# A fp32 decoder layer on one core: stored permuted identity for the keys, new first loads and first rotation, row-block-first end

## What is computed

```python
h = rmsnorm(x, attn_norm)
qkv = einsum('bsd,de->bse', h, w_in)            # (256,1024) x (1024,3072)
q, k = rope(q), rope(k)
o_moba = moba_attention(q[:8 heads], ...)       # one block of 256 keys: causal attention
o_dil = dilated_mixture(q[8 heads:], ...)       # three dilated windows, mixed by denominators
mixed = concat(rmsnorm(o_moba), rmsnorm(o_dil))
x = x + mixed @ w_out
h = rmsnorm(x, ffn_norm)
x = x + (silu(h @ w_gate) * (h @ w_up)) @ w_down
out = rmsnorm(x, final_norm)
```

## Time and profile before

| what | us |
|---|---|
| median of three runs (lowest, highest) | 311.64 (311.19, 312.02) |
| the profiled execution: its own time | 311.84 |
| its span, first to last instruction | 309.9 |
| TensorE busy with matmuls | 301.3 (97%) |
| VectorE busy | 200.7 (65%) |
| ScalarE busy | 170.8 (55%) |
| GpSimd busy | 10.3 (3%) |
| TensorE's share of the chain that ended last | 96% |
| moved by DMA | 61.59 MB, 199 GB/s on average |

### The profile page before, as it was taken

The page is one execution under the profiler, slowest core; times in us unless marked ns, Lnnn a source line. Parts: engine busy times, 40 slices in busy tenths (PEclk is TensorE's granted clock), DMA queues, the critical chain, the costliest instruction groups (busy, mean ns, idle before and its releaser), DMA issues.

```text
span 309.9 us, 4293 instructions
## 1 busy us (share of the span) xinstructions
PE 301.3 (97%) x1430; PEld 246.1 (79%) x1430; DVE 200.7 (65%) x323; ACT 170.8 (55%) x294; POOL 10.3 (3%) x24
## 2 busy tenths in 40 slices
PE   7999999999999999999999999999999999999991
PEld 3788877788888988888888888888888888888880
DVE  3677979997877388855757374656565555555425
ACT  4785563968678458746453443526354444444224
POOL 0001000000020020200000000000000000000002
PEclk9999999999999999999999999999999999999998
DMA  6997635568482355482985656565657474561003
GB/s 200 390 410 298 222 111 161 189 185 286 116 285 71 144 170 237 153 316 78 347 326 170 224 183 210 187 223 176 252 170 270 161 256 174 209 220 31 0 0 135
DMA packets 22332, 61.59 MB, mean 199 GB/s; under 512 B 2608, under 2 KB 14000, under 8 KB 16432
## 3 DMA queue, kind: packets, MB, share of 16 engines
q1 hardware_dynamic: 22032, 60.89, 56.2%
q10 hardware_dynamic: 288, 0.54, 0.5%
HBM read 54.60 MB, written 1.05 MB: 180 GB/s over the span
## 4 chain that ended last, share of the span: by engine, by line
PE 96%; DMA 1%; ACT 1%; DVE 0%; POOLq 0%; issue 0%; POOL 0%
PE bank L403 30%; PE bank L404 29%; PE bank L405 29%; PE bank L471 3%; PE bank L430 2%; DMA gain<-in_gains 1%; PE bank L451 1%; PE bank L481 1%; PE bank L454 1%; PE bank L413 1%; PE bank L455 0%; PE bank L456 0%; POOLq L193 0%; ACT junk L667 0%; ACT rot L811 0%; DVE w_lo L851 0%
## 5 line engine op out<-in xcount | busy, mean ns | idle before, releaser
L636 ACT ACTIVATE w_hi<-raw 128x1024 fp32r<-128x1024 f32 x94 | 97.9, 1057 | 81.8 <-PE bank L405 71.9
L831 DVE TENSOR_TENSOR w_lo<-raw,w_hi 128x1024 fp32r<-128x1024 f32 x94 | 111.8, 1214 | 18.8 <-ACT w_hi L636 17.3
L403 PE MATMUL bank<-w_hi,x_hi 128*128 128x512 f32 x272 | 109.0, 401 | 0.8 <-DVE w_lo L851 0.8
L404 PE MATMUL bank<-w_lo,x_hi 128*128 128x512 f32 x272 | 106.6, 392 | 0.0
L405 PE MATMUL bank<-w_hi,x_lo 128*128 128x512 f32 x272 | 106.5, 392 | 0.0
L403 PEld LDWEIGHTS bank<-w_hi,x_hi 128*128 128x128 f32 x272 | 51.5, 189 | 13.1 <-DVE w_lo L851 2.2
L405 PEld LDWEIGHTS bank<-w_hi,x_lo 128*128 128x128 f32 x272 | 51.5, 189 | 11.1
L404 PEld LDWEIGHTS bank<-w_lo,x_hi 128*128 128x128 f32 x272 | 51.6, 190 | 10.1
L403 PE MATMUL bank<-w_hi,h_hi 128*128 128x512 f32 x80 | 31.2, 390 | 0.0
L405 PE MATMUL bank<-w_hi,h_lo 128*128 128x512 f32 x80 | 31.1, 389 | 0.0
L404 PE MATMUL bank<-w_lo,h_hi 128*128 128x512 f32 x80 | 31.1, 389 | 0.0
(11 more groups left out here) (75 smaller groups left out, 233.9 us busy)
## 6 DMA issues: line engine op xcount, KB each, us to landing
raw<-in_weights SPq DMA_DIRECT2D x46, 1024.0 KB, 4.8
landed<-p_squares SPq DMA_DIRECT2D x88, 64.0 KB, 2.1
raw<-in_weights SPq DMA_DIRECT2D x5, 512.0 KB, 9.1
o_sb<-in_x_turned SPq DMA_DIRECT2D x4, 256.0 KB, 7.0
xs<-in_x SPq DMA_DIRECT2D x2, 512.0 KB, 8.5
out<-rot SPq DMA_DIRECT2D x4, 256.0 KB, 2.0
raw<-in_weights SPq DMA_DIRECT2D x2, 256.0 KB, 4.1
vals<-in_final_norm ACTq DMA_DIRECT2D x1, 512.0 KB, 7.2
```

The costliest lines, as they stand in the source:

```text
L403: pe.matmul(dst, a_hi, w1, start=first, stop=False)
L404: pe.matmul(dst, a_hi, w2, start=False, stop=False)
L636: act.activation(w_hi[:, slot:slot + 2, :], raw[:, slot:slot + 2, :], ACT.Copy).then_inc(hi_ready, 1)
L831: dve.tensor_tensor(w_lo[:, slot:slot + 2, :], raw[:, slot:slot + 2, :], w_hi[:, slot:slot + 2, :].bitcast(f32), ALU.subtract).then_inc(lo ...
```

## The change

Four things change.

1. **Keys** are turned by a unit matrix that is stored permuted in the table (`C_KEYS`), read with stride one. The table's first load grows from 384 to 512 columns.
2. **First loads.** x arrives in five pieces (1, 1, 2, 2, 2 row blocks), weights 2 and 3 one by one. The q, k, v blocks run in a new order: (j, k) = (0,0), (1,0), (0,1), (1,1), then k = 2 to 7 of j = 0, k = 2 to 7 of j = 1, then the rest as before. VectorE makes x_hi of row block 0, ScalarE begins with w_hi of blocks 0 and 1; the first block's six matmuls are ordered hi·hi, lo·hi, hi·lo over both halves, each with its own wait. Nine warm-up matmuls instead of ten. The table is loaded ahead of the fourth quad.
3. **First rotation.** The queries of group 0 are rotated with the plain table, both halves at once after the tenth block; ScalarE scales `rot` by 1/rms afterwards (item "scale"), and TensorE's turn waits for that.
4. **The last quarter.** Of chunk 9's down blocks six three_passes run, with the turn after three. Then chunk 10's for s = 0 left, s = 0 right, s = 1 left. The last quarter (s = 1, right 512 columns) runs as two halves of 256 columns, each with chunk 9's and chunk 10's blocks: the left into bank 3, the right into bank 7. VectorE adds, and sums the squares of the last 256 columns itself on top of the other sums (`tensor_tensor_reduce`); GpSimd takes only the power. ScalarE's own queue writes the quarter s = 1 left.

```diff
-WARM = 10
+WARM = 9
+SHARED = 2
+QKV_ORDER = ([(j, k) for k in range(SHARED) for j in range(2)]
+             + [(j, k) for j in range(2) for k in range(SHARED, KT)]
+             + [(j, k) for j in range(2, 6) for k in range(KT)])
+XT_LOADS = (0, 1), (1, 2), (2, 4), (4, 6), (6, 8)
+X_AFTER = 1, 3, 4, 6
-FIRST_LOADS = {0: 1, 1: 1, 2: 2, 4: 2, 6: 2, 8: 2, 10: 2}
+FIRST_LOADS = {0: 1, 1: 1, 2: 1, 3: 1, 4: 2, 6: 2, 8: 2, 10: 2}
 DVE_PLAN = {
-    8: [("rope", 0, 0, 0)],
-    11: [("rope", 0, 0, 1)],
...
+    9: [("rope", 0, 0, 0), ("rope", 0, 0, 1)],
...
 ACT_PLAN = {
-    14: [("turn", 0, 0, 0)],
+    11: [("scale", 0), ("scale", 1)],
+    16: [("turn", 0, 0, 0)],
...
-        ident_ja = ident.rearrange("p (a j) -> p j a", j=JS)
+        ident_ja = tab[:, C_KEYS:C_KEYS + P]
...
+            sp.dma_start(tab[:, 0:C_MASK], table[:, 0:C_MASK]).then_inc(in_tab, 16)
             sp.wait_ge(lo_ready, 2)
             quad(NQ, 0)
             for s in range(SH):
                 sp.dma_start(xs[:, s, :], x[0, s * P:(s + 1) * P, :]).then_inc(in_x[s], 16)
-            sp.dma_start(tab[:, 0:C_MASK], table[:, 0:C_MASK]).then_inc(in_tab, 16)
...
+            def first_block():
+
+                pe.wait_ge(x0_hi, 1)
+                pe.wait_ge(hi_single, 1)
+                for s in range(SH):
+                    pe.matmul(bank[s][:], x_hi[:, 0, s * P:(s + 1) * P], w_hi[:, 0, :], start=True, stop=False)
+                pe.wait_ge(xt_lo, 1)
...
+                for cols, dst in ((slice(0, NH), bank[3]), (slice(NH, NB), bank[7])):
+                    for i, (parts, t) in enumerate((p, t) for p in (old, new) for t in range(FT)):
+                        slot = (GU_BLOCKS if parts is old else 0) + 2 * t + 1
+                        ins = three_pass(dst[:, cols], parts[0][:, t * SH + 1, :], parts[1][:, t * SH + 1, :], slot,
+                                         dst is bank[7] and i == 0, i == 2 * FT - 1, cols)
+                    ins.then_inc(end_done, 1)
...
+            add_end(1, 1, right, 5, bank[7])
+            last = xs[:, 1, NB + NH:2 * NB]
+            dve.wait_ge(res_done, 14)
+            dve.wait_ge(ms_end, 1)
+            dve.tensor_tensor_reduce(out=normed[:, 1, 1, right], in0=last, in1=last, scale=1.0 / D_MODEL,
+                                     scalar=ms[:, 0:1], op0=ALU.mult, op1=ALU.add,
+                                     accum_out=ms[:, 1:2]).then_inc(ms_end, 1)
             dve.wait_ge(rstd_ready, rstd_count["final"] + 1)
...
+            pool.tensor_tensor(rstd[:, 9:10], ms[:, 1:2], neg_half[:, 9:10], ALU.pow).then_inc(rstd_ready, 1)
```

More of the change, by code:

```diff
@@ L400, in _, with three_pass @@
         def _(pe):
-            def three_pass(dst, a_hi, a_lo, slot, first, last):
-                w1, w2 = w_hi[:, slot, :], w_lo[:, slot, :]
+            def three_pass(dst, a_hi, a_lo, slot, first, last, cols=slice(0, NB)):
+                w1, w2 = w_hi[:, slot, cols], w_lo[:, slot, cols]
                 pe.matmul(dst, a_hi, w1, start=first, stop=False)
@@ L489, in item @@
                     x_turn(n)
+            def first_block():
[4 more added lines that the diff above has]
+                pe.wait_ge(xt_lo, 1)
+                for s in range(SH):
+                    pe.matmul(bank[s][:], x_lo[:, 0, s * P:(s + 1) * P], w_hi[:, 0, :], start=False, stop=False)
+                pe.wait_ge(lo_single, 1)
+                for s in range(SH):
+                    ins = pe.matmul(bank[s][:], x_hi[:, 0, s * P:(s + 1) * P], w_lo[:, 0, :], start=False, stop=False)
+                ins.then_inc(blk_done, 1)
             def qkv_block(i):
-                j, k = i // KT, i % KT
+                j, k = QKV_ORDER[i]
+                if i == 0:
+                    first_block()
+                    return
                 if i < SINGLES:
                     pe.wait_ge(*((lo_ready, i // 2 + 1) if i % 2 else (lo_single, i // 2 + 1)))
-                elif k % 2 == 0:
+                elif i % 2 == 0:
                     pe.wait_ge(lo_ready, i // 2 + 1)
@@ L557, in turn_last_hidden, with down_part, down @@
                 ins.then_inc(ht_pe, 1)
-            def down(c, pair0, slot0, first, last):
+            end_parts = [o[:, 0:FT, :].rearrange("p a (s b) -> p (a s) b", b=P) for o in (o_hi, o_lo)]
+            def down_part(parts, t, n, s, slot, first, last):
+                return three_pass(bank[2 * n + s][:], parts[0][:, t * SH + s, :], parts[1][:, t * SH + s, :],
+                                  slot + 2 * t + n, first, last)
+            def down(c, pair0, slot0, first):
                 for t in range(FT):
@@ L583, in step @@
                             gate_up(k, s, k)
-                down(c - 1, pair0 + GU_BLOCKS // 2, GU_BLOCKS, first, last)
+                if last:
+                    last_downs()
+                else:
+                    down(c - 1, pair0 + GU_BLOCKS // 2, GU_BLOCKS, first)
             def first_chunk(k, s):
@@ L1032, in _, with add_end @@
-            for n in range(2):
-                with_gain(1, n)
-            dve.wait_ge(rstd_ready, rstd_count["final"] + 1)
-            dve.wait_ge(gained, 3)
-            dve.tensor_scalar(normed[:, 1, 0, :], normed[:, 1, 0, :], rstd[:, 9:10], None, ALU.mult).then_inc(fin_dve, 1)
+            def add_end(s, n, cols, done, src):
+                at = slice(n * NB + cols.start, n * NB + cols.stop)
+                dve.wait_ge(end_done, done)
+                dve.tensor_tensor(xs[:, s, at], src[:, cols], xs[:, s, at], ALU.add).then_inc(res_done, 1)
@@ new lines, in with_gain @@
+            def with_gain(s, n, cols, done):
+                at = slice(n * NB + cols.start, n * NB + cols.stop)
+                dve.wait_ge(res_done, done)
+                dve.tensor_tensor(normed[:, s, n, cols], xs[:, s, at], gain_out[:, at], ALU.mult).then_inc(gained, 1)
+            full, left, right = slice(0, NB), slice(0, NH), slice(NH, NB)
+            dve.wait_ge(in_gout, 16)
+            add_end(0, 0, full, 1, bank[0])
+            with_gain(0, 0, full, 9)
+            add_end(0, 1, full, 2, bank[2])
@@ new lines, in _ @@
+            with_gain(0, 1, full, 10)
+            add_end(1, 0, full, 3, bank[1])
+            with_gain(1, 0, full, 11)
+            add_end(1, 1, left, 4, bank[3])
+            add_end(1, 1, right, 4, bank[3])
+            with_gain(1, 1, left, 12)
+            dve.wait_ge(sq_done, 14)
+            dve.tensor_scalar(ms[:, 0:1], ssq[:, 9:10], ssq2[:, 9:10], EPS, ALU.add, ALU.add).then_inc(ms_end, 1)
+            dve.wait_ge(res_done, 13)
+            add_end(1, 1, right, 5, bank[7])
+            last = xs[:, 1, NB + NH:2 * NB]
```

190 lines of the change are left out of this document (114 added, 76 removed).

## The result

| | before | changed |
|---|---|---|
| time, us, median (range) | 311.80 (311.19 to 312.02) | 308.24 (308.12 to 308.47) |
| ratio to before, 95% interval | 1 | 0.989 [0.987, 0.991] |
| profiled execution / span | 311.84 / 309.86 | 308.24 / 306.36 |
| block 4's first matmul | 13.80 | 12.73 |
| from there to the end of the last matmul | 289.55 | 287.82 |

The kernel before was run again beside the changed one. One of the changed kernel's four runs took 337.46 us at a mean granted clock of 0.85 and is left out here and in the ratio; with it the median is 308.36. Forecast were 308.2 us and a range of 306.9 to 310.0. The span is 3.50 us shorter: 1.07 at the head, 1.73 between block 4 and the last matmul, 0.70 in the tail. A second set of runs, on another chip, gave 307.86 against 312.03, ratio 0.986 [0.984, 0.989].

A forecast was written before the change was run, and what follows sets the result against it. TensorE, busy almost throughout the middle, was taken as the bound, plus head and tail. Terms -1.92 - 0.8 + 0.16 - 0.85 = -3.41 us took the profiled 311.84 to 308.4, forecast 308.2 as median, range 306.9 to 310.0.

The forecast's parts named there:

- Keys: Keys' transposes on TensorE: with stride one, four turns fall from 0.92 to 0.44 us each, -1.92 us.
- Head: Start up to block 4: 256 KB less ahead of weights 4-5, block 4 at 13.0; -0.8 us, bounds 0 and -1.5.
- the place of block 4 counts, not that of block 0: Start: block 4's place sets the kernel's end; an earlier first matmul, 0.9 us sooner, alone is worth nothing.
- block 4 waits for its load with either clock: Start: block 4 is held by its weights' load whether the clock rises early or late.
- if the clock rises where it did: Start: condition for block 2 starting at about 10.3 and block 4 at 13.0, with the first matmul at 5.5.
- the sum keeps its value: Clock's rise at the start: its run-to-run variation leaves the total forecast of -3.41 us unchanged.
- Warm-up: Before block 0: nine matmuls end at 5.2, closing the hole before the first real one; costed at nothing.
- Rotation: First rotation of the queries: VectorE starts at 21.2, pair 8 begins at 25.4; cost nothing.
- Halves: Last quarter: 24 matmuls of 256 columns, 0.12 us apart, replace 12 of 512; +0.16 us, bounds 0 and +1.84.
- rival 4: Middle turns: VectorE and ScalarE cannot follow the earlier TensorE, up to 1 us comes back, 309.2 us; chance 0.08.
- Tail: Last matmul to span end: 5.4 to 5.8 us against 6.5; -0.85 us, bounds -0.5 and -1.1.
- rival 5: Start: clock stays at 1.2 GHz, block 4 at 15.6; about 312.9 us if the rise comes at 20; chance 0.03.

The follow-up runs named there:

- warm12_tail: tail_order with 12 warm-up matmuls instead of nine; 308.04 us, ratio to before 0.988.
- pair23: Changed kernel with weights 2 and 3 as one load of 512 KB, x of row blocks 2 and 3 behind it; 308.73 us, ratio to before 0.990.
- first_block_old: Changed kernel with block 0 written as all others, waiting for all its inputs before the first matmul; 308.53 us, ratio to before 0.990.
- keys_only: Kernel before with only the stored permuted unit matrix for the keys; 310.34 us, ratio to before 0.996.
- block_order: Changed kernel with the old order of the first twelve blocks and x again loaded ahead of the weights that need it; 309.53 us, ratio to before 0.992.
- rotation_old: Changed kernel with the first rotation of the queries as before: scaled table, two places on VectorE, no ScalarE scaling; 308.45 us, ratio to before 0.989.
- tail_order: Changed kernel with ScalarE's squares of the third quarter ahead of the first quarter's scaling; 308.39 us, ratio to before 0.988; second set 307.67 us, 0.985.

## Why the prediction was right, and where it was not

**Keys: right.** 1.8 of 1.92 us, by two kernels. The Trainium skill (SBUF — State Buffer, Door 1: The DMA port swizzle) would have fp32 strided by 4 for free. The trace doesn't agree for a moving operand read with a stride of four elements, 16 bytes: 0.12 us on a transpose of 128 columns, 0.23 against 0.11 us. Its other half, a penalty for each new line of 16 bytes, does agree.

**Head: the size within the bounds, the reason wrong.** The step that failed is "the place of block 4 counts, not that of block 0", with "block 4 waits for its load with either clock". In nine of the ten profiles with the changed kernel's loads block 4 didn't wait for its weights, and in the tenth, warm12_tail, by 0.03 us. With an early clock the last wait is as a rule block 2's, for weights that are the last of the first 1024 KB; pair23 shows that a delay there goes through. In first_block_old and warm12_tail these weights were so early that block 2 didn't wait either. With a late clock TensorE didn't wait at all once block 0 had begun: 5.83, 8.53, 10.52, 13.25 are matmuls at 0.43 us and then at 0.23. Block 2 at 10.3 "if the clock rises where it did" was near that (10.52). The landing of weights 4 was forecast at 11.4 (12.34 less 0.94) and was 10.6 to 11.4 in the ten; on average 10.87, against 12.35 in the three profiles with 2304 KB to load up to there (before, keys_only, block_order). So the 256 KB were worth 1.5 us rather than 0.94, and that is why block 4 no longer waited. At a like clock the head gives 0.45 to 0.55 us (late: 13.80 to 13.25 and 13.35) or 0.7 to 1.1 (early: keys_only's 13.45 to 12.73 and 12.39; rotation_old, where weights 2 came latest, has 13.10); the 1.07 of the two traces compare a late clock with an early one. The 0.8 lies among these by luck. So does the start of block 0: in ten profiles with the new first block it comes 0.77 or 0.78 us after ScalarE takes weights 0, which from the 5.03 of the old trace would be 5.8 and not 5.5. The 5.53 came with weights at 4.75, and the ten go from 5.53 to 6.20.

**The sentence on the clock.** The Trainium skill (TensorE: Matmul & The Clock Gate, What's actually happening) says that the moment of the rise varies from run to run, by 500 ns to either side. The runs agree that it varies, but by more: 4.97 to 9.82 us in one head. The prediction drew from it that the sum keeps its value; it doesn't: block 4 starts 0.5 to 0.9 us later with the late rise.

**Warm-up.** That one less costs nothing was not tried by itself; none at all cost 1.0 us.

**Rotation: right**, it cost nothing, and by rotation_old it even saves the 0.17 us wait of block 16. The times on VectorE were too early: the rotation starts at 22.53 (21.2 forecast) and pair 8 at 26.60 (25.4), which still leaves over 1 us ahead of block 16. That the table's new place costs nothing was not tried by itself; no wait of TensorE shows there.

**Halves: right.** Spacing 0.12 as forecast, +0.21 us measured for +0.16. Of the last hidden values' turn no wait came. Rule and row part here: by the Trainium skill (TensorE: Matmul & The Clock Gate, Back-to-back issue gap) a matmul of 256 columns would follow after 109 ns; the rows show 120. The prediction's "-0.10" by that rule took the rule for the halves and the trace for the whole ones; with the rule for both, as an estimate, 24 x 109 - 12 x 216 ns is +0.02 us.

**The sum in the middle.** Keys -1.79, halves +0.21, the wait of block 16 that the new rotation saves -0.13: -1.71, where -1.73 was measured and -1.76 forecast. No wait of rival 4 appeared in the changed kernel; warm12_tail shows that it had little room.

**Tail: 0.70 of 0.85 us.** The chain from the add on was as forecast: with the power at 0.54 us the two issues stand 2.4 us behind the start of the add, and 3.05 us pass from there to the end (2.7 to 3.1). But the add starts 0.38 us behind the last matmul, so the issues are at 2.8 us and not at 2.4. What was not seen is that the add stands on VectorE behind an operation that waits for ScalarE's squares, and these behind a scaling put too early: tail_order takes 0.27 of the 0.38 us back. That the tail still ended at the edge of its 5.4 to 5.8 us is luck: the sum allowed 0.88 us for the power, and the 0.34 us by which it was quicker paid for most of the wait.

**Two small slips.** In rival 5 block 4 would start at 15.4 us by its own terms (10.3 + 5.1), not 15.6; and the last matmul before ended at 303.35, 0.04 us ahead of the add, not 0.02. Neither moves the forecast.

## What to carry to other kernels

Measure a head's gain at like states of the clock: two profiles of one program can differ by more than the edit, so look at the spacing of the first matmuls before a difference is put down to a load. When loads are moved ahead, follow which block waits last; it changes, and what was "nothing" (a first block's start) may begin to count. In a tail, write down for each engine what stands ahead of the last chain's operations: a wait on a small helper operation costs as much as one on the chain.
